# Fetching each expert's dot row and value row as one 8 KB run in the latent streams

## The reference, cut to what matters

```python
expert = i1 * PEER_KEYS + i2
w = jax.nn.softmax(best_s, axis=-1)
...
u = jnp.take(u_tab, ec, axis=0)
act = jax.nn.gelu(jnp.einsum('cd,ced->ce', hc, u), approximate=False)
v = jnp.take(v_tab, ec, axis=0)
return jnp.einsum('ce,ced->cd', (act * wc).astype(h.dtype), v)
```

## Time and profile before

| | us |
|---|---|
| median of 3 runs | 3064.56 |
| lowest, highest | 3058.0, 3065.03 |
| span of the profiled execution, from its first to its last instruction | 3264.9 |

### The profile page before, as it was taken

How to read it: one execution, slowest core, us unless ns; L and a number is a source line. 1 busy time by engine, 2 the same in 40 slices (tenths; PEclk the granted TensorE clock), 3 DMA queues, 4 the chain that set the end, 5 groups by cost and what they waited for, 6 DMA issues and landing times. The chain is left out here.

```text
span 3264.9 us, 25886 instructions
## 1 busy us (share of the span) xinstructions
PE 2484.1 (76%) x8511; PEld 1388.6 (43%) x8511; DVE 2109.8 (65%) x4293; ACT 530.3 (16%) x1177; POOL 1599.1 (49%) x1633
## 2 busy tenths in 40 slices
PE   5985688988688899789577677677887676667775
PEld 2663365656245666566322222232565222222222
DVE  0649679888739878785877654425377776844444
ACT  1130111000002000123211112111142111111111
POOL 1100435766424666330666666666212666666664
PEclk8997887999887999898798898898899789988988
DMA  6528999999978999830999999999613999999997
GB/s 248 207 91 350 397 385 343 405 408 403 358 279 323 380 413 402 314 130 29 348 371 356 346 409 366 356 342 368 250 33 130 370 357 358 342 354 375 363 375 294
DMA packets 254920, 1038.80 MB, mean 318 GB/s; under 512 B 34923, under 2 KB 36818, under 8 KB 238660
## 3 DMA queue, kind: packets, MB, share of 16 engines
q0 software_dynamic: 221184, 805.40, 64.5%
q1 hardware_dynamic: 31528, 229.28, 17.6%
q10 hardware_dynamic: 2076, 2.47, 0.3%
HBM read 1032.61 MB, written 4.44 MB: 318 GB/s over the span
## 5 line engine op out<-in xcount | busy, mean ns | idle before, releaser
L1901 PE MATMUL PS<-W,SCALE 128*128 128x512 f32 x1952 | 1004.1, 661 | 443.8 <-issue 297.2
L1901 PEld LDWEIGHTS PS<-W,SCALE 128*128 128x128 f32 x1952 | 384.9, 209 | 1058.7 <-issue 989.7
L2007 DVE CUSTOM_DVE_ANT_0 W<-W,PS 128x1024 f32<-128x1024 f32 x512 | 599.8, 1217 | 198.2 <-DMA W<-in_peer_u,IDX 157.9
L2045 POOL DMA_INDIRECT W<-in_peer_u,IDX x512 | 485.2, 948 | 467.4 <-DVE IDX L1127 241.6
L2045 POOL DMA_INDIRECT W<-in_peer_v,IDX x512 | 490.7, 958 | 297.5 <-issue 133.8
L1741 POOL DMA_INDIRECT ROWS<-in_peer_u,IDX x206 | 211.7, 1028 | 429.1 <-issue 297.6
L1951 ACT ACTIVATE SCALE<-C,COEF 128x128 f32<-128x128 f32 x488 | 184.6, 398 | 1157.1 <-PE PS L1901 421.0
L1396 PE MATMUL PS<-XT,W 128*128 128x256 f32 x1408 | 307.3, 380 | 0.0
L1396 PEld LDWEIGHTS PS<-XT,W 128*128 128x128 f32 x1408 | 268.3, 191 | 45.1 <-issue 10.5
L1741 POOL DMA_INDIRECT ROWS<-in_peer_v,IDX x184 | 208.2, 1131 | 115.8 <-issue 48.6
L313 PE MATMUL PS<-W,XT 128*128 128x512 f32 (+2 forms) x576 | 222.6, 545 | 26.5 <-issue 20.6
(11 more groups left out here) (293 smaller groups left out, 2565.7 us busy)
## 6 DMA issues: line engine op xcount, KB each, us to landing
W<-in_w_mod SPq DMA_DIRECT2D x12, 4096.0 KB, 14.3
W<-in_w_up SPq DMA_DIRECT2D x44, 1024.0 KB
W<-in_w_in SPq DMA_DIRECT2D x21, 2048.0 KB, 10.9
W<-in_w_down SPq DMA_DIRECT2D x22, 1024.0 KB
W<-in_peer_wq SPq DMA_DIRECT2D x6, 2048.0 KB, 11.0
W<-in_w_o SPq DMA_DIRECT2D x6, 2048.0 KB
W<-in_w_out SPq DMA_DIRECT2D x4, 2048.0 KB
W<-in_peer_u,IDX POOLq DMA_INDIRECT x512
```

Of the source, the lines that this page charges most:

```text
L1901: ins = nc.tensor.matmul(PS[:, 4 + 2 * t + h, :], SCALE[:, i % NSCALE, :], row_slot(at[1, g])[:, h * 512:(h + 1) * 512], start=m == 0, sto ...
L2007: nc.vector.tensor_tensor_reduce(row_slot(n), row_slot(n), h_of(t), 1.0, 0.0, ALU.mult, ALU.add, DOT[:, t, m:m + 1]).then_inc(rows_used, 1)
L2045: nc.gpsimd.indirect_dma_start(row_slot(n), None, tables[("peer_u_2", "peer_v_2")[v]], bass.IndirectOffsetOnAxis(IDX[:, t, m:m + 1], 0),). ...
```

## The change

The host lays the two tables side by side in one, so that an expert's dot row and value row are one run of 8 KB. The latent streams fetch that run with one indirect DMA per pick: 256 fetches per layer in place of 512. The ring has eight slots of 8 KB (`PAIRS2` = 8) in the same memory. A slot is free again when the matmul of its value row is done. `LAG`, `TAIL`, `ORDER` and `UNIT` go: dot, gelu, scale matrix and matmul of a row follow one another. ScalarE takes gelu of one column per row. VectorE writes the scale matrix of row n - 1 after the dot of row n, in one `tensor_scalar` with two scalars (gelu(dot) and softmax weight), so `COEF` is not needed for it. TensorE adds all rows. The searches take one head at a time and spread to row 183; the steps for layer 1's keys move to rows 200 to 236. The context streams read the same joint table as single rows of 4 KB, with indices 2e and 2e + 1 (a second index tile `IDXV`, one more small operation per search).

```diff
-RING2 = 16
+PAIRS2 = 8
 NSCALE = 4
...
+        one_by_one = A["peer_uv_2"].rearrange("l n (c d) -> (l n c) d", c=2)
+        in_pairs = A["peer_uv_2"].rearrange("l n e -> (l n) e")
...
+        def pair_slot(n):
+            return W[:, n % PAIRS2 // 2, n % 2 * 2 * D:(n % 2 + 1) * 2 * D]
...
-        KEYS_STEP = {144: 0, 168: 1, 236: 2, 252: 3}
-        KEYS_AT = {7: 1, 33: 2, 49: 3, 65: 4, 81: 5, 97: 6, 113: 7}
-        PAIRS_AT = {15: 1, 41: 2, 57: 3, 73: 4, 89: 5, 105: 6, 121: 7}
+        KEYS_COLS, KEYS_ROWS, KEYS_PROJ, KEYS_TURN = 202, 212, 217, 236
+        KEYS_ROOT7, KEYS_ROOT8 = 204, 227
+        KEYS_STEP = {200: 0, 208: 1, 223: 2, 231: 3}
+        SEARCH_AT = {3 + 20 * c // 3: (2 + c // 2, c % 2) for c in range(2 * (TT * EH - 2))}
+        SOFTMAX_AT = {32 * (k - 1) - 6: k for k in range(2, len(FOUND))}
+        SPREAD_AT = {32 * (k - 1) - 2: k for k in range(2, len(FOUND))}
...
TensorE:
+                            pair_in(pe, l, n)
+                            pe.wait_ge(scale_ready, n + 1)
                             for h in range(2):
+                                ins = nc.tensor.matmul(PS[:, 4 + 2 * t + h, :], SCALE[:, n % NSCALE, :],
+                                                       v_of(n)[:, h * 512:(h + 1) * 512], start=m == 0,
+                                                       stop=m == PICKS - 1, skip_group_check=True)
                             ins.then_inc(scaled_rows_used, 1)
...
ScalarE:
                         softmax(0)
+                        softmax(1)
+                        for n in range(TT * PICKS):
...
+                            if n in SOFTMAX_AT:
+                                softmax(SOFTMAX_AT[n])
+                            one = slice(m, m + 1)
+                            act.wait_ge(rows_used, n + 1)
+                            nc.scalar.activation(DOT[:, t, one], DOT[:, t, one], ACT.Gelu).then_inc(gelu_ready, 1)
...
VectorE:
+                        def scale(n):
+                            t, m = divmod(n, PICKS)
+                            one = slice(m, m + 1)
+                            if n >= NSCALE:
+                                dve.wait_ge(scaled_rows_used, n - NSCALE + 1)
+                            dve.wait_ge(weights_spread, group_of(n) + 1)
+                            dve.wait_ge(gelu_ready, n + 1)
+                            nc.vector.tensor_scalar(SCALE[:, n % NSCALE, :], ident, DOT[:, t, one], WGT[:, t, one], ALU.mult, ALU.mult
+                                                    ).then_inc(scale_ready, 1)
...
+                            pair_in(dve, l, n)
+                            nc.vector.tensor_tensor_reduce(u_of(n), u_of(n), h_of(t), 1.0, 0.0, ALU.mult, ALU.add, DOT[:, t, m:m + 1]
+                                                           ).then_inc(rows_used, 1)
+                            if n >= 1:
+                                scale(n - 1)
+                            if n < 2:
+                                softmax_tail(*FOUND[n], n)
+                            if n in SPREAD_AT:
+                                softmax_tail(*FOUND[SPREAD_AT[n]], SPREAD_AT[n])
+                            if n in SEARCH_AT:
+                                search(*SEARCH_AT[n])
+                            if n == PICKS + 6:
                                 onto_stream(0)
...
GpSimd:
+                            if n == PAIRS2 // 2:
                                 pool.wait_ge(groups_done, groups.of("pq", TT - 1, 0))
+                            if n == PAIRS2 * 3 // 4:
                                 pool.wait_ge(groups_done, groups.of("pq", TT - 1, 1))
+                            if m % TOPK == 0:
+                                pool.wait_ge(picks_ready, n // TOPK + 1)
+                            if n >= PAIRS2:
+                                pool.wait_ge(scaled_rows_used, n - PAIRS2 + 1)
                             nc.gpsimd.indirect_dma_start(
+                                pair_slot(n), None, in_pairs, bass.IndirectOffsetOnAxis(IDX[:, t, m:m + 1], 0),
+                            ).then_inc(pair_landed[n % PAIRS2], 16)
```

More of the change, by code:

```diff
@@ L162, in program @@
         row_landed = [sem(f"row_landed{i}") for i in range(BESIDE)]
-        row_landed2 = [sem(f"row_landed2_{i}") for i in range(RING2)]
+        pair_landed = [sem(f"pair_landed{i}") for i in range(PAIRS2)]
         first_loaded = [sem(f"first_loaded{i}") for i in range(WS)]
@@ L224, in program @@
         coef_ready = sem("coef_ready")
+        weights_spread = sem("weights_spread")
         scaled_rows_used = sem("scaled_rows_used")
@@ L1937, in _ @@
+                        for n in range(TT * PICKS):
+                            t, m = divmod(n, PICKS)
+                            if l == 0 and n == KEYS_ROOT7:
                                 root(act, TT, 7, 1.0 / D, 1)
-                            if l == 0 and g == KEYS_ROWS_V:
+                            if l == 0 and n == KEYS_ROWS:
                                 keys_act_rows(act, groups, B)
-                            if l == 0 and g == KEYS_PROJ_V:
+                            if l == 0 and n == KEYS_PROJ:
@@ new lines, in _ @@
+                        for h in range(2):
+                            search(h, 0)
+                            search(h, 1)
+                        for n in range(TT * PICKS):
+                            t, m = divmod(n, PICKS)
+                            if m == 0:
+                                dve.wait_ge(h_copied, t + 1)
+                            pair_in(dve, l, n)
[10 more added lines that the diff above has]
+                            if n == PICKS + 6:
@@ L2017, in _ @@
                                 onto_stream(0)
-                            if l == 0 and g in KEYS_STEP:
-                                keys_dve(dve, link, groups, B, statistic, inverse, KEYS_STEP[g])
+                            if l == 0 and n in KEYS_STEP:
+                                keys_dve(dve, link, groups, B, statistic, inverse, KEYS_STEP[n])
+                        scale(TT * PICKS - 1)
                         onto_stream(1)
@@ L2155 @@
     given.update(chunked(given))
+    for name in ("peer_u_2", "peer_v_2"):
+        del given[name]
     given.update(constants())
```

182 lines of the change are left out of this document (41 added, 141 removed).

## The result

The changed kernel takes 3071.5 us (median of 20 runs) and the kernel before 3064.3 (20 runs): ratio 1.0018, 95% interval 1.0009 to 1.0026. It is 7 us, or 0.2%, slower. The ratio leaves out one slow execution of the changed kernel, of 7041.8 us. The profiled execution took 3071.06 us, its span is 3069.3.

The account below looks back on a forecast made before the run. The prediction took the DMA engines' pace in the two latent streams as the bound, POOL's issuing close behind. Terms -58 + 16 + 0 + 0 + 5 = -37 us took 3064.56 to 3028 us, range 2965 to 3100.

Parts of the forecast that it names:

- Term 4: Ring's slack in the latent streams: less slack set against faster refilling and no lock step, 0; bounds -100 to +86 us.
- Term 1: Transfers of the latent streams: joint 8 KB runs save 0.114 us per pair, -58 us; bounds 0 and 150 saved.
- Term 2: Start of each layer's stream: first slot freed late, a gap of 8 us per layer, +16 us in all.
- Term 5: Layer 1's keys beside layer 0's stream: 7 us delay against 7.4 of slack, nearly hidden, +5 us; bounds 0 and 15.
- Term 3: VectorE's added scale matrices: 2.27 us of the 2.63 per pair while searching, hidden by the transfer, cost 0.
- B: Rival: ring too short, VectorE's searches exceed the 7.4 us of slack; 86 us lost, 3114 us; chance 0.17.
- D: Rival: DMA gaps close as POOL is no longer at its limit, half of 100 us gained, 2978 us; chance 0.21.
- C: Rival: runs are cut into 4 KB packets or scattered 8 KB runs move no faster, 3086 us; chance 0.07.
- E: Rival: VectorE sets the pace while it searches, 41 us of the transfer gain lost, 3069 us; chance 0.10.
- F: Rival: VectorE and GpSimd exclude each other at SBUF, scale matrices wait for fetches, +209 us, 3237 us; chance 0.04.

Follow-up runs that it names:

- b_again: The kernel before, unchanged, profiled a second time, on a chip where it takes 3064 us: own time 3065.91 us, span 3064.1.
- c_start: Changed kernel with ScalarE's exp of heads 0 and 1 ahead of tile 1's read-outs: 3106.3 us (ratio 0.957 to before), where before takes 3244.4.
- the split: Changed kernel with each pair search cut in two: 3096.1 us where before takes 3249.6, 3058.8 us where before takes 3062.5.
- d_after: The changed kernel as it is, on a chip where before takes 3249.6 us: 3106.2 us, ratio 0.9568 to before.
- two4k: Changed kernel with each pair fetched as two 4 KB runs: 3273.2 us where before takes 3267.3; ratio 1.012 where before takes about 3064.
- the combination: Changed kernel with early exp, ten slots in layer 1, ScalarE's scale matrices, split searches: 3042.2 us (before 3062.5), 3079.2 us (before 3249.6).

## Why the prediction was wrong

**Which steps failed.** Of the 38 us between the forecast -37 and the +1 that the terms come to below, 24 are Term 4, put at 0 where it costs 24, and 24 are Term 1, put at -58 where the wire gives 34; Terms 2 and 5 cost 8 and 2 less than forecast. Term 4 came to 0 only because the short ring's loss was set against gaps that would close, and those gaps are of another chip than the median. That is the last sentence of the sum: "it lies 200 us above the median of 3064.56, so the profile stretches what it records. I carry the difference over". The profile stretches nothing: spans and own times of the same execution differ by 2 us. The kernel before loses 201 us more in the profile with the span of 3264.9 than in b_again, 42 ahead of the first latent fetch, 75 and 81 in the two streams, 3 between them. On a chip of that kind the change brings 143 us, on the chips of the median it costs 7; 37 us faster is right for neither. That 3071.5 lies inside the stated range of 2965 to 3100 is owed to the range's width, not to the account. A sign was there: many of the gaps of the earlier trace rows ended with "remote", which nothing in the program explains, and the gaps of the earlier trace rows summed to 100 us per execution.

Term by term, for the first kind:

- **Term 1**, -58. The direction was right, the size was off: the wire gives 0.067 us per pair, -34 us. The 428 GB/s of the weight loads aren't reached by scattered runs of the same length: 420. And the 382.5 GB/s from which the 58 was taken belong to the second kind: on the first the same queue holds 805.40 MB in 66.6% of 3064.1 us, 395 GB/s, and the hardware queue 229.28 MB in 18.7%, 400. By these two the same sum would have given some 19 us.
- **Term 2**, +16. The mechanism was right, the size twice too large: VectorE waits 16.21 us for the first exp, and the first value row comes late and slowly (three rows in 7.00 us, against 1.96 for one). In the first 40 us of layer 0's stream 294 against 243 GB/s is 2.0 MB, 5.0 us; in layer 1, 322 against 233 GB/s from 2375 to 2420 is 9.8 us, 6.5 of which are the later first fetch. So +8. VectorE's first exp, TensorE's first three rows, and POOL's fetch of row 8 at the start of layer 0:

```profile
1528.05 0.17 DVE L1151 TENSOR_REDUCE SUM<-EI 128x1 f32<-128x16 f32 x1 [16.21 <-ACT EI L897]
```

```profile
1530.23 7.00 PE L1898 MATMUL PS<-W,SCALE 128*128 128x512 f32 x12 [5.89 <-DVE SCALE L1967]
```

```profile
1534.07 0.94 POOL L2012 DMA_INDIRECT W<-in_peer_uv,IDX  x1 [9.12 <-PE PS L1898]
```

 The early exp mended little of it: VectorE then waits 12 us for the first gelu, which stands behind the same read-outs (c_start, second kind).
- **Term 3**, 0. Right as to VectorE's load: 389.10 busy of 460 us (85%) while searching against 2.27 / 2.63 = 86% forecast, and it paces nothing by its sum. But "hidden by the transfer, cost 0" looks at VectorE's load alone; its scale matrix, behind the next row's dot, is also part of every slot's round. ScalarE writing it brought some 14 us on the second kind; the sum here counts that in Term 4.
- **Term 4**, 0. Wrong: it costs 366 x 0.067 = 24 us, all that the wire gives on the rows beside searches (409 GB/s there, 420 after them). By the working (7.4 us of slack less a burst of 6.65) the ring would just hold. But POOL's pause is longer than VectorE's burst: 7.81 us above, up to 9.1 in layer 1 from 2430 to 2850 us. And the rest was set against a gain that the first kind doesn't have. And "the lock step of coefficient, gelu and scale at 24 rows' distance is gone" was counted as a relief; that distance was the cover. In before, value rows go on being added, and their slots go on coming free, through a 10.6 us search, as the lines above show; afterwards all eight slots wait for VectorE. Three edits that leave the packets alone show the cause: six slots cost 184 us, ten bring 420 GB/s beside the searches of layer 1, and the split alone brings 10 us on either kind.
- **Term 5**, +5. The end of a layer has grown by 1.5 us: from the start of the last row's work to `X`, 2183.42 to 2189.82 before and 2186.81 to 2194.70 after, since the last matmuls wait for two rows' scale matrices (a pair of rows in 3.67 us). Twice that is +3 (layer 1's end was taken to be the same). The steps for layer 1's keys left no mark that before lacks: 392 GB/s beside them before and 404 after, 17 and 16 below the quiet rows.

The sum of these is -34 + 8 + 24 + 3 = +1, and the profiled executions differ by 5; 1.7 of the rest lie in the dense part between the streams, the other 2 or 3 I can't place.

**The rivals.** B had the mechanism and the deciding point, at a quarter of its price (24 us of 86), 28 searches at 0.9 us each; its sign, a share under 0.92, did not come with eight slots (1.00). D was right for the second kind, and had reckoned with half: layer 0's stream shrinks from 763.6 to 693.6 us, layer 1's from 759.1 to 675.8 (rows' profile against d_after). They are then as long as on the first kind (693.2, 677.0), so all the gaps close. C is refuted (420 against 409), E too: with the same VectorE load the split kernel moves 413 GB/s at 2600 to 2700 us and the one with ten slots 420. F predicted VectorE waiting for fetches before each scale matrix; it doesn't, on either kind (20.8 us of idle time before all 512 on the first). By the rule of the Trainium skill named with F (SBUF — State Buffer, "Who interferes with whom") VectorE and GpSimd take turns where a VectorE instruction uses the port pair that they share, and TensorE and ScalarE never wait for anyone. The MAX8 above, one per fetch, look like such turns, but ScalarE and TensorE stood still as well, and the first kind runs the same instructions without a pause. So that rule alone doesn't explain the standstills; whether it has a part in them isn't shown.

**Open.** What differs between the chips is not shown. Each of the five chips was used once, with 11 to 17 executions of before, all of one kind, so it isn't shown either that a chip stays of its kind. Shown is that in the latent streams the standstills come with two 4 KB fetches per pair (two4k: 0.2% from before) and go with one of 8 KB. That edit changes two things at once, how often POOL issues and how many packets there are of which length. The theory of the standstills blames POOL's unbroken issuing; that the 4 KB packets do it was not ruled out. Fetching the 8 KB runs with two instructions of 64 tokens each, which leaves the packets as they are, would help to tell. The 29 us by which the changed kernel's first latent fetch comes later on the second kind arise in the standstills at 863 to 921 us shown above. Not tried were the combination without the early exp, and a larger ring in layer 0, where one of the two tiles is needed for layer 1's keys.

## What to carry to other kernels

Compare the span of a profile with the time of its own run before anything is built on its gaps. If they are 6% apart, the profile is of another chip or state, and its gaps may not be those of the execution that was timed. Waits that end with "issue" or "remote" after several us were the warning here. When steps at a distance are joined into one chain, ask what released buffers while the busiest engine was away; the longest burst of that engine, not its mean load, set here how deep the ring had to be. If a burst doesn't fit, cutting it in two is a cheap cure (10 us here, with the same 4943 VectorE instructions).

## What the runs showed that I had not expected

- Chips of one type differ by 6% on the same kernel (3063 to 3065 on some, 3244 to 3267 on others), and by 1% on a kernel with half the fetch instructions in its two latent streams (3071 and 3106); most of that 1% arises in 60 us of the context streams, which still fetch 4 KB rows.
- Scattered runs of 8 KB move 420 GB/s at a full queue, of 4 KB 409, and consecutive loads 428.
- A short ring doesn't show in the DMA share at first: at a share of 1.00 the rate was 409 GB/s in place of 420, and only the slices of 2.5 us show the dips.
